# Four of six groups of conditioning weights on GpSimd instead of TensorE, and keys first in the first head pair

## The reference, cut to what matters

```
def adaln(cond, w, b):
    m = jax.nn.silu(cond) @ w + b
    return jnp.split(m, 6, axis=-1)
...
sh_m, sc_m, g_m, sh_f, sc_f, g_f = adaln(c[:, None, :], ada_w[i], ada_b[i])
...
csh_m, csc_m, cg_m, csh_f, csc_f, cg_f = adaln(c_ctx[None, None, :], ada_w[i], ada_b[i])
```

## Time and profile before

| what | us |
|---|---|
| median of three runs | 1669.47 |
| the profiled execution's own time | 1667.93 |
| its span in the trace | 1666.0 |
| TensorE busy in the span | 1505.8 |
| VectorE busy | 542.1 |
| ScalarE busy | 233.9 |
| GpSimd busy | 73.4 |

### The profile page before, as it was taken

One profiled execution on the slowest core, in us unless ns is written; L12 is line 12 of the kernel. 1 busy time (PEld: TensorE's weight loads), 2 busy tenths in 40 slices (PEclk: granted clock), 3 DMA queues, 4 the chain that ended last, 5 costly groups with the idle time before them and its releaser, 6 DMA issues.

```text
span 1666.0 us, 15126 instructions
## 1 busy us (share of the span) xinstructions
PE 1505.8 (90%) x6382; PEld 630.0 (38%) x6382; DVE 542.1 (33%) x976; ACT 233.9 (14%) x426; POOL 73.4 (4%) x58
## 2 busy tenths in 40 slices
PE   4989999998959999988898899999499999988897
PEld 2544555545423333332233344444233333333232
DVE  1145464641542323232232421112612323222232
ACT  3133343421310000000000200003200000000000
POOL 0001100100010000000000040000000000000000
PEclk9999999999979999999999999999699999999999
DMA  9432414388169999999999932121599999999997
GB/s 375 131 152 101 167 69 169 116 340 352 43 262 428 427 425 426 428 427 426 426 427 428 397 130 87 65 97 80 202 381 426 426 427 427 427 426 427 426 427 298
DMA packets 56061, 504.90 MB, mean 303 GB/s; under 512 B 7631, under 2 KB 7854, under 8 KB 25018
## 3 DMA queue, kind: packets, MB, share of 16 engines
q1 hardware_dynamic: 51744, 490.68, 71.2%
q0 software_dynamic: 2752, 8.92, 1.5%
q10 hardware_dynamic: 1498, 4.33, 0.7%
HBM read 497.62 MB, written 6.29 MB: 302 GB/s over the span
## 4 chain that ended last, share of the span: by engine, by line
PE 65%; DMA 28%; DVE 4%; issue 1%; ACT 1%; ACTq 0%; DVEq 0%; POOLq 0%
PE ps L789 24%; PE ps L870 10%; DMA ring<-in_exp_w_up_dram 7%; DMA work<-in_exp_w_up_dram 7%; PE ps L684 6%; DMA ring<-in_exp_w_gate_dram 5%; DMA work<-in_exp_w_gate_dram 5%; PE ps L803 3%; PE ps L606 3%; PE ps L461 3%; PE ps L574 3%; PE ps L513 3%; PE ps L517 2%; PE ps L388 2%; PE ps L592 2%
## 5 line engine op out<-in xcount | busy, mean ns | idle before, releaser
L789 PE MATMUL ps<-ring,work 128*64 128x512 f32 x2016 | 452.8, 598 | 38.4 <-DMA ring<-in_exp_w_gate_dram 15.6
L789 PEld LDWEIGHTS ps<-ring,work 128*64 128x64 f32 x2016 | 140.8, 137 | 331.1 <-issue 277.4
L789 PE MATMUL ps<-work 128*64 128x512 f32 x1056 | 239.3, 601 | 23.3 <-DMA work<-in_exp_w_gate_dram 9.0
L1506 DVE TENSOR_TENSOR work<-ps,work 128x1024 f32<-128x1024 f32 x120 | 141.3, 1219 | 288.7 <-PE ps L803 288.7
L789 PEld LDWEIGHTS ps<-work 128*64 128x64 f32 x1056 | 74.1, 138 | 177.3 <-issue 144.4
L803 PE MATMUL ps<-work 64*128 64x512 f32 x480 | 119.2, 615 | 0.0
L1086 ACT ACTIVATE work<-ps 128x512 f32<-128x512 f32 x32 | 19.1, 597 | 510.8 <-PE ps L789 510.8
L1524 DVE SCALAR_TENSOR_TENSOR work<-ps,gate_e,gate_ffn 128x512 f32<-128x512 f32 x32 | 24.0, 751 | 185.8 <-PE ps L789 185.8
L1517 DVE TENSOR_TENSOR work<-work,ps 128x512 f32<-128x512 f32 x32 | 22.0, 688 | 189.4 <-issue 156.8
L870 PE MATMUL ps<-ring 128*128 128x512 f32 x192 | 82.6, 592 | 0.0
L870 PE MATMUL ps<-ring,work 128*128 128x512 f32 x192 | 82.6, 592 | 0.0
(11 more groups left out here) (247 smaller groups left out, 1191.3 us busy)
## 6 DMA issues: line engine op xcount, KB each, us to landing
ring<-in_exp_w_up_dram SPq DMA_DIRECT2D x42, 2048.0 KB, 32.9
ring<-in_exp_w_down_dram SPq DMA_DIRECT2D x42, 2048.0 KB, 37.1
ring<-in_exp_w_gate_dram SPq DMA_DIRECT2D x42, 2048.0 KB, 32.0
ring<-in_ada_w_dram SPq DMA_DIRECT2D x22, 2048.0 KB, 7.4
work<-in_exp_w_gate_dram SPq DMA_DIRECT2D x22, 2048.0 KB, 36.1
work<-in_exp_w_up_dram SPq DMA_DIRECT2D x22, 2048.0 KB, 33.7
work<-in_exp_w_down_dram SPq DMA_DIRECT2D x22, 2048.0 KB, 33.7
ring<-in_conv_w_in_dram SPq DMA_DIRECT2D x3, 2048.0 KB, 32.0
```

The costliest lines, as they stand in the source:

```text
L789: last = mm(PS[64 * h:64 * h + 64, bank, :], lhsT[:, m * P + 64 * j:m * P + 64 * j + 64], slot_rows[sl][:, m, h * BANK:(h + 1) * BANK], st ...
L1506: v.tensor_tensor(row, PS[:, b:b + 2, :], row, ALU.add).then_inc(added[L], 1)
```

## The change

- Groups 1 to 4 are no longer multiplied on TensorE. GpSimd does them from the low-rank stage on, in 32 slices of 128 rows (1 MB each): four instructions of 512 columns multiply the slice by its 128 values of the condition (one value for each partition), and, but for the first slice of a group, four more add it to the group's sum in SBUF. TensorE then sums over the partitions in `acc_collect` with matmuls by a column of ones: 512-wide ones for gates, sixteen 128-column ones with a single moving column for shift and scale.
- The last group stays on TensorE: 4 units, in the last pair.
- Slices 0 and 1 are loaded ahead of the attention weights; slice n is loaded when slice n-2 is done. The units of the last group are loaded behind the last slice and behind projection 40; output weights half 0 behind slice 32, chunks 0 and 1 behind units 3 and 4, output weights half 1 behind the collection of group 4.
- GpSimd's part of turning q and scaling k goes to VectorE. Each `turn_q` there has six operations of 256 columns, and a scaling of 768 columns is added.
- The low-rank latents are no longer copied first: ScalarE squares and VectorE scales straight from PSUM; the key gain is multiplied per tile, and the copy back is gone.
- The first pair's order is keys (4 to 9), then queries, turns 3 to 7, 0, 1, the collection of group 1, turn 2.
- The row maximum is written to PSUM instead of SBUF. Rings 0 and 2 change roles.

The core of the diff:

```diff
+            for n in range(2, SLICES):
+                sp.wait_ge(slice_added, n - 1)
+                load_slice(n)
+            sp.wait_ge(proj, 10 * PAIRS)
+            for u in range(UNITS):
+                if u >= 2:
+                    sp.wait_ge(unit_mm, u - 1)
...
+            def acc_collect(c):
+                part = GROUPS[c][1]
+                acc_c = ada_acc[c % 2]
+                pe.wait_ge(slice_added, KC * c)
+                for g in range(4):
+                    cols = acc_c[:, g * BANK:(g + 1) * BANK]
+                    n, half = (4 * part + g) // 2, g % 2
+                    if n % 3 == 2 and n // 3 == 0:
+                        last = mm(PS[:, GATE_BANKS[c][half], :], ones.to_broadcast([P, P]), cols, start=True, stop=True)
...
+                        for q in range(4):
+                            block = cols[:, q * P:(q + 1) * P] if n // 3 == 0 else quarter(cols, q)
+                            last = mm(PS[:, MOD_BANK[c], 4 * g + q:4 * g + q + 1], block, ones, start=True, stop=True)
...
                     project(i + 1, 4)
                     project(i + 1, 5)
+                    if i >= 1:
+                        pe.wait_ge(proj_d, 5 * i + 8)
+                        pe.wait_ge(pT_a, 8 * i + 4)
+                        acc_collect(1 + i)
                     scores(3)
                     probs_T(2)
-                    project(i + 1, 6, u)
-                    project(i + 1, 7, u)
-                    unit(u)
-                    project(i + 1, 8, u + 1)
-                    project(i + 1, 9, u + 1)
-                    turn(i + 1, range(0, 3))
-                    unit(u + 1)
+                    for s in range(6, 10):
+                        project(i + 1, s)
+                    turn(i + 1, (0, 1, 2))
                     values(0)
                     probs_T(3)
-                    unit(u + 2)
-                    turn(i + 1, range(3, 8))
-                    pe.wait_ge(trn_a, 4 * i + 8)
-                    pe.wait_ge(unit_added, KC // 2 * (i + 1))
-                    ada_collect(i + 1)
+                    turn(i + 1, (3, 4, 5, 6, 7))
                     values(1)
-                    unit(u + 3)
...
-            v.tensor_copy(krot[:, CT:NT, :], kraw[:, CT:NT, :]).then_inc(krot_ready, 1)
+            v.tensor_tensor(r4[:, :, :, 1, :], tm[0], tm[1], ALU.add).then_inc(krot_ready, 1)
...
                     if ahead and t == 2:
                         take(i + 1, 5)
+                        if i >= 1:
+                            ada_take(1 + i)
+                        gain_q(i + 1)
                         turn_q(i + 1)
...
+            pool.wait_ge(setup_out, 1)
+            for n in range(SLICES):
+                c, k = 1 + n // KC, n % KC
+                total = ada_acc[c % 2]
+                pool.wait_ge(unit_in[n % 2], 16 * (n // 2 + 1))
+                if k == 0 and c >= 3:
+                    pool.wait_ge(ada_sum, c - 1)
+                part = ada_slice[n % 2]
+                for q in range(4):
+                    cols = slice(q * BANK, (q + 1) * BANK)
+                    last = g.tensor_scalar((part, total)[k == 0][:, cols], part[:, cols], cond_T[:, k, 0:1], None, ALU.mult)
+                if k >= 1:
+                    last.then_inc(slice_scaled, 1)
+                    pool.wait_ge(slice_scaled, n - n // KC)
+                    pool.wait_ge(slice_added, n)
+                    for q in range(4):
+                        cols = slice(q * BANK, (q + 1) * BANK)
+                        last = g.tensor_tensor(total[:, cols], part[:, cols], total[:, cols], ALU.add)
+                last.then_inc(slice_added, 1)
```

More of the change, by code:

```diff
@@ L403, in ada_collect @@
                     last = tr(PS[:, MOD_BANK[c], q * P:(q + 1) * P], cols, ident)
-                if part == 1:
-                    for h in range(2):
-                        last = mm(PS[:, GATE_BANKS[c][h], :], ident[:, 32 * h:32 * h + 1].to_broadcast([P, P]), sums,
-                                  start=True, stop=True)
                 if part == 2:
@@ L649, in pair @@
                     scores(3)
                     probs_T(2)
-                    unit(u + 4)
                     values(0)
                     probs_T(3)
+                    pe.wait_ge(pT_a, 8 * PAIRS)
+                    acc_collect(LAST - 1)
                     values(1)
-            for s in range(8):
-                project(0, s, 0)
-            unit(0)
-            project(0, 8, 1)
-            project(0, 9, 1)
-            turn(0, range(0, 3))
-            unit(1)
-            unit(2)
@@ L664, in _ @@
-            turn(0, range(3, 8))
+            for s in (4, 5, 6, 7, 8, 9, 0, 1, 2, 3):
+                project(0, s)
+            turn(0, (3, 4, 5, 6, 7, 0, 1))
+            acc_collect(1)
+            turn(0, (2,))
             for i in range(PAIRS):
@@ L1026, in pair @@
                 take_o(1)
-            for s in range(0, 8, 2):
-                take(0, s)
-                if s in (0, 2):
-                    square_q(0, s // 2)
+            take(0, 4)
+            take(0, 6)
             square_k(0, 0)
             take(0, 8)
-            take_T(0, 0)
             square_k(0, 1)
-            take_T(0, 2)
-            root(0)
-            f(stat[:, 95:96], eps, ACT.Exp)
+            root_k(0)
+            take(0, 0)
+            square_q(0, 0)
+            take(0, 2)
+            square_q(0, 1)
             take_T(0, 4)
             take_T(0, 6)
+            take_T(0, 0)
+            root_q(0)
+            f(stat[:, 95:96], eps, ACT.Exp)
+            take_T(0, 2)
             for i in range(PAIRS):
@@ L1119, in _ @@
             v.memset(eps, EPS).then_inc(consts, 1)
+            v.memset(ones, 1.0)
             dve.wait_ge(consts, 1)
@@ L1287, in pair @@
             def pair(i):
-                u = UNIT_AT[i + 1]
                 ahead = i + 1 < PAIRS
```

368 lines of the change are left out of this document (177 added, 191 removed).

## The result

The changed kernel takes **1726.14 us** (median of four runs, 1725.44 to 1727.34) against 1669.16 before (four runs, 1668.7 to 1669.74). The ratio is 1.0342, with a 95% interval of 1.0324 to 1.036: slower by 57.0 us, where 1667.5 had been forecast and the range ended at 1685. The profiled execution took 1725.44 us, its span is 1723.4, the mean granted clock 0.952.

The account below looks back on a forecast made before the run. TensorE's path from 93 to 388 us was taken as the bound. Terms 3.4 + 3.1 - 3.7 - 0.2 - 5.6 + 0.4 + 0.6 = -2.0 us on 1669.47 gave 1667.5; range 1646 to 1685.

Parts of the forecast that it names:

- GpSimd's pace: GpSimd's slices: 0.60 us a multiplication and 1.10 an addition, so 7.1 us a slice and group 4 done near 300 us.
- All three signs: Wrong if GpSimd's multiplication costs over 0.75 us, TensorE waits for `slice_added`, or x lands over 16 us behind the last values.
- Rival B: GpSimd becomes the bound: at 1.10 us a multiplication, slices take 9.1 us; +16 against the forecast, about 1684; chance 0.25.
- turns slower from about 0.75 us: GpSimd's multiplication: the duration from which the changed kernel was expected to become slower.
- The path to SBUF: VectorE and GpSimd share one path, held to an instruction's end: VectorE waits 0.85 us following another operation, about half at random.
- Rival A: The shared path hardly costs, VectorE often gets in at once: -27 without waits, 1642.4, half of it 1655; chance 0.27.
- The divisions' cover: VectorE's softmax divisions: waits costed at nothing, with 2 us of slack at the first tile and more later.
- Behind the low-rank stage: Before the first projection: copies and key gain go, -1.3; six small turns wait for GpSimd, +4.7; sum +3.4 us.
- I take 3.0: A collection's eight narrow matmuls on TensorE: 0.16 to 0.4 us each; with two wide ones 3.0 to 4.9 us, taken as 3.0.
- the five terms before the first scores: From low-rank stage to first scores: 20.9, 3, 2.5, 2.5 and 2.5 us, given as 31.6 against 35.0 before.
- Rival C: The gain is not passed on: x comes later by what the pairs gain, 1669 to 1671 us; chance 0.08.
- The clock: Two new TensorE stands of 5.3 us may bring the slow clock, 0 to 2.4 us each; taken 0.3 each, +0.6.

Follow-up runs that it names:

- e_ts7: Changed kernel with GpSimd's additions replaced by one-input multiplications, both multiplications of 225 of 512 columns, sums left out: 1660.59 us.
- e_mul_only: Changed kernel with GpSimd's multiplications 512 columns wide but its additions only 8, sums left undone: 1663.75 us.
- e_narrow: Changed kernel with each GpSimd instruction touching 8 columns instead of 512, all waits kept, sums of groups 1 to 4 undone: 1662.62 us.
- e_mul_tt: Changed kernel with GpSimd's multiplication as a two-input instruction, the condition spread along the row, same result: 1694.67 us.
- e_ts9: Changed kernel with GpSimd's additions replaced by one-input multiplications, both multiplications of 324 of 512 columns, sums left out: 1662.18 us.
- e_ts11: Changed kernel with GpSimd's four additions a slice replaced by one-input multiplications of 386 of 512 columns, sums not formed: 1724.21 us.
- e_wide: Changed kernel with one multiplication and one addition of 2048 columns a slice instead of four and four of 512: 1741.82 us.
- e_lowrank: Kernel before, with only latents squared and scaled straight from PSUM, key gain per tile and no copy back: 1667.58 us, ratio 0.9988.
- e_pace7: e_narrow with 32 memsets of 63 columns behind each slice's multiplications (16 in a group's first slice): 1662.25 us.
- e_slice7: e_narrow with 104 memsets of 19 columns behind each slice's multiplications: 1657.41 us.
- e_add_only: Changed kernel with GpSimd's additions 512 columns wide but its multiplications only 8: 1669.52 us.
- e_quarter: e_narrow with only one in four of the single-column matmuls left in the collections of groups 2, 3 and 4: 1645.8 us.

## Why the prediction was wrong

**The step that failed is GpSimd's pace:** "I take 0.60, since it also has one input", with bounds of 0.49 and 1.10. The multiplication took 1.55 us. Both bounds were wrong in kind: the lower was another engine's, and the upper rested on the idea that one input can't cost more than two. The earlier trace rows bound only the addition, and that one was near: 1.24 to 1.26 against 1.10. From there on the argument followed its own number to a false end. A slice took 11.2 us and not 7.1; group 1, which was to be "in time", was waited for by 6.0 us; "TensorE does not wait for its sums" became a wait of 14.6; and the units came 28 us late. At 6.9 to 7.1 us a slice (e_ts7, e_mul_only) there is in fact no wait, as the prediction said of its own pace. All three signs that it had named for being wrong came true: a multiplication over 0.75 us, waits for slices, and, in e_narrow, an x that lands 17.3 us behind the last values.

**Rival B was right in kind and not in price.** It named the multiplication as what decides, and a multiplication over 0.75 us as what would prove the forecast wrong. Its +16 came at 1.10 us and mostly from longer waits of VectorE. With the two-input form at a slice of 9.1 (e_mul_tt) that mechanism is real, and the kernel takes 27.0 us more than the one before; with the one-input form at 8.8 (e_ts9) it takes 6.2 less. These 33 us between the two are what the forecast's waits and B's surcharge make together (25 and 8). The forecast's "turns slower from about 0.75 us" was too early for the pace as such: 0.96 us (a slice of 8.8 less an addition of 1.24, four of each) is still harmless, 1.55 is not. B had no case in which slices themselves, and the units behind them, came late; that case makes 50.3 of the 57 us.

**The path to SBUF:** the wait of 0.85 us an operation, the mean length of a GpSimd instruction, holds in kind for GpSimd's additions (turns of 1.37 to 1.48 us in place of 0.42). It doesn't hold beside TENSOR_SCALAR: where all of GpSimd's instructions are of this form (e_ts11), a turn of line 1272 took 0.83 us at most and 0.62 in the median. The rule of the Trainium skill (SBUF — State Buffer, Who interferes with whom), by which a second SBUF input meets GpSimd and the loser fully blocks, agrees for additions (1.48 us for a turn) and for the division beside a long multiplication (2.16 us). For two-input instructions beside a multiplication the trace agrees in part: they are held for the first 3.6 of its 5.4 us in e_wide, and not for the rest. Rival A had named this case ("one-input instructions that leave the read side early"). The divisions' cover, costed at nothing, held: their median was 0.74 us.

**GPSIMD Engine Reference (section 4.1)** of the Trainium skill, weighed in the prediction at an estimated 0.43 us a multiplication, is contradicted here by a factor of 3.6. Its advice in 3.1 to use VectorE for elementwise work is borne out: the multiplication of 512 columns takes 1.55 us on GpSimd, and one took 0.49 on VectorE.

**Behind the low-rank stage:** +3.4 forecast, +3.7 measured (102.5 against 98.9). This was partly luck. The copies and the gain that go were to bring 1.3 us, and e_lowrank, which has only them, starts 0.5 later (99.3 against 98.9). The turns were to wait 4.7 us and cost 3.2: the three operations at lines 1227 to 1229 took 1.35, 1.23 and 1.23 us in place of 0.29, the other three hardly waited.

**Without waits the change gains 5 us and not 27.** Against rival A's terms, e_narrow shows first scores +2.1 (A: -4.7), pair 0 -10.6 (-10.3), pair 1 -2.6 (-6.9), pair 2 -0.8 (-5.6), pair 3 +3.3, and x +2.6 (x lands 17.3 us behind the last values, 14.7 before). Other kernels in which TensorE waits for no slice lie 4.8 (e_mul_only), 6.2 (e_ts9), 6.9 (e_pace7), 7.7 (e_ts7) and, with an early start, 13.8 us (e_slice7) below the one before: none reaches the 27. A good part is one term of the sum, the collection: "I take 3.0". It takes 5.9 us in pair 1 of e_narrow (3.90, and 1.98 for its two gate halves), 4.7 in pair 2, 5.5 in the last pair of the changed kernel (1.98 + 3.50), and 7.0 for the sixteen single-column matmuls of group 3 at the slow clock. One of eight in a group costs 0.46 to 0.49 us, more than the 0.4 taken as the upper end, one of group 3's sixteen 0.29. The lower end, 0.16 for a turned block, misread, where eight records of 1.09 us are four blocks, 0.27 each. And behind each collection comes a stretch at the slow clock, 1.6 to 2.4 us in e_narrow, which the sum did not have. (A slip of 0.2 us adds to this: the five terms before the first scores make 31.4 and not 31.6.) So even at 0.60 a multiplication the forecast would have leaned on a sum that had the collections too cheap. No run has its own case, four multiplications of 0.60 and four additions a slice. The nearest are e_ts7, 7.7 us below the kernel before (no additions), and e_add_only, 1.0 above (its turns met no addition); the forecast was -2.0. Rival C's mechanism shows too, at 2.6 us: x follows the last values at a greater distance, and takes that much of what the pairs gain.

**The clock** was put at +0.6, for two stands of TensorE; e_narrow alone loses 5.6 us to it behind its collections. In the changed kernel the last collection is followed by values of 8.2 us, at a granted clock of 0.50 at first, where e_quarter has 5.4. The mean granted clock from 300 to 400 us fell from 1.00 to 0.73 (TensorE busy for 51.5 of 100 us, 93.4 before), so TensorE did part of its work at the lower level, 1.2 GHz, behind the long waits: a collection's 32 records took 6.96 us behind the 14.6 us wait and 4.66 in e_narrow. The changed kernel takes 63.5 us more than e_narrow, 13 more than its three waits; that is the slow clock together with the waits of VectorE, and no run takes the two apart. In e_ts11, without additions, the three waits make 57.1 of the 62.0 us above e_ts9, which leaves 5 for the clock and the rest.

## What to carry to other kernels

Before work is moved to an engine, the duration of exactly that instruction form on exactly that engine is the term that decides; a row of another engine, or of another form, is not a bound on it, and the range should have been widened until a measured row was in it. A producer that feeds a fixed order costs nothing until it is late and then costs its whole lateness: from 8.8 to 11.3 us a slice, GpSimd's last slice ends 72 us later (404.5 against 332.4), and 62 of these came out in the time. Look also for who stands behind it in a queue: 28.4 us of the loss were spent waiting not for GpSimd's sums but for loads that SyncE issued behind its slices, and by the estimate above nearly all of that is their place in the order.

## What the runs showed of the hardware

- GpSimd's TENSOR_SCALAR with one value for each partition is slower than its TENSOR_TENSOR for the same 512 fp32 columns: 1.55 us against 1.25 (addition) and 1.04 (multiplication with the value broadcast as the second input). It took 1.25 us for 386 columns, 1.09 for 324, 0.84 for 225 and 0.30 for 8: 2.5 ns a column and 0.28 us.
- Which VectorE instruction GpSimd holds, and for how long, depends on both forms. GpSimd's TENSOR_TENSOR holds VectorE's two-input turns to its end (1.37 to 1.49 us for 0.42, 4.61 in e_wide) and its division too (4.67 for 0.62 in e_wide). TENSOR_SCALAR holds the division to its end (2.16 for 0.62 in e_wide), but two-input instructions only at first: in e_wide until 3.6 us after its start (2.69 for 0.68, 2.92 for 0.29), and for the rest of its 5.4 us they ran at their own 0.28 to 0.42. Operations that read PSUM took their usual time (line 1308: 0.74).
- Behind sixteen to thirty-two records of matmuls with a single moving column (3.5 to 4.7 us in which the trace shows TensorE busy) the granted clock fell to its lower level: 0.51 from 295.5 to 300.5 us in e_narrow, and 1.00 in e_quarter, with a quarter of them.
- A row of back-to-back memsets of 9 columns held one division of VectorE for 8.2 us, to the end of the row: it got no turn between the memsets.
- One execution ran every matmul five times slower, 3.0 us for 512 columns, with the granted clock shown as 1.0.
